# Four-strip bias table products ahead of the transposes, and a new order of dilated loads and first values, in a hybrid decoder step on one Trainium2 core

## The reference, cut to what matters

```python
h = rms_norm(x, norm_attn); proj = h @ w_in          # 2840 columns
bias = rel_bias[t5_bucket(distance)]                 # (32, 16 heads), log buckets
# mixer A, sample rows: windows (128, 1), (512, 4), (2048, 16) over the cached keys and values
logits = q . k * scale + bias; probs = masked_softmax(logits); out = probs @ v
# mixer B, sample rows: compressed blocks -> top 16 blocks -> gathered keys and values -> softmax -> @ v
x = x + concat(A, B) @ w_out; y = final_norm(x + conv_ffn(rms_norm(x, norm_ffn)))
```

## Time and profile before

| what | value |
|---|---|
| median of 3 runs | 2094.52 us (2089.33 to 2097.07) |
| the profiled execution | 2091.84 us |
| its span | 2090.0 us |
| TensorE busy | 2030.1 us (97%), 12334 matmul records |
| VectorE, ScalarE, POOL busy | 53%, 25%, 28% |
| DMA | 373.04 MB moved, 178 GB/s on average |

### The profile page before, as it was taken

How to read it: one execution, slowest core, us unless ns; L and a number is a source line. 1 busy time by engine, 2 the same in 40 slices (tenths; PEclk the granted TensorE clock), 3 DMA queues, 4 the chain that set the end, 5 groups by cost and what they waited for, 6 DMA issues and landing times. The chain is left out here.

```text
span 2090.0 us, 31740 instructions
## 1 busy us (share of the span) xinstructions
PE 2030.1 (97%) x12334; PEld 1325.8 (63%) x12334; DVE 1113.5 (53%) x2524; ACT 520.4 (25%) x1140; POOL 578.9 (28%) x753
## 2 busy tenths in 40 slices
PE   7999999999989989999999999999999999999998
PEld 3445466666556666766776458888888888634443
DVE  4035455421535546777775467777776766511452
ACT  4111010101333435776675031111111111000001
POOL 2444234202025740112232441322222222304110
PEclk9999999999999999999999999999999999999999
DMA  9376677663699994233343126666665422601111
GB/s 255 118 237 258 263 289 277 242 214 124 229 365 387 419 409 162 70 92 92 93 143 112 29 81 221 221 211 213 218 205 202 142 81 62 242 4 30 43 40 41
DMA packets 154296, 373.04 MB, mean 178 GB/s; under 512 B 34885, under 2 KB 92989, under 8 KB 136093
## 3 DMA queue, kind: packets, MB, share of 16 engines
q1 hardware_dynamic: 126420, 149.63, 22.8%
q0 software_dynamic: 25472, 149.45, 18.4%
q10 hardware_dynamic: 2256, 71.94, 9.8%
HBM read 343.68 MB, written 98.60 MB: 212 GB/s over the span
## 5 line engine op out<-in xcount | busy, mean ns | idle before, releaser
L2981 PE MATMUL ff_ps<-ff_hx,whole_aw 128*128 128x264 f32 x2464 | 550.5, 386 | 0.8 <-DVE ff_hx L3377 0.8
L2981 PEld LDWEIGHTS ff_ps<-ff_hx,whole_aw 128*128 128x128 f32 x2464 | 467.1, 190 | 80.6 <-issue 1.2
L837 DVE STREAM_TRANSPOSE whole_space<-whole_space 128x512 f32<-128x512 f32 x256 | 155.3, 674 | 153.6 <-PE late_bank L637 153.6
L601 PE MATMUL late_bank<-in_w,in_xT 128*128 128x512 f32 (+1 forms) x512 | 201.6, 547 | 0.0
L1224 DVE CUSTOM_DVE_ANT_0 pa_L<-late_bank,whole_space 128x512 f32<-128x512 f32 (+3 forms) x288 | 141.0, 532 | 43.4 <-PE late_bank L1070 41.8
L601 PEld LDWEIGHTS late_bank<-in_w,in_xT 128*128 128x128 f32 x512 | 95.1, 191 | 95.0 <-issue 88.4
L1196 ACT ACTIVATE pa_L<-pa_L,pa_nm 128x640 f32<-128x640 f32 (+3 forms) x192 | 142.0, 741 | 47.0 <-DVE pa_nm L1236 46.7
L3007 PE MATMUL ff_ps<-ff_hx,whole_space 128*128 128x512 f32 x336 | 148.0, 593 | 0.0
L717 ACT ACTIVATE in_yout<-late_bank 128x128 f32<-128x128 f32 (+5 forms) x88 | 40.9, 479 | 380.7 <-PE late_bank L601 200.2
L3461 DVE SCALAR_TENSOR_TENSOR whole_space<-whole_space,ff_kept 128x1024 f32<-128x1024 f32 x88 | 123.1, 1399 | 3.1
L637 PE MATMUL late_bank<-whole_space 128*64 128x256 f32 (+1 forms) x1152 | 121.6, 364 | 0.0
(11 more groups left out here) (441 smaller groups left out, 2670.0 us busy)
## 6 DMA issues: line engine op xcount, KB each, us to landing
out_new_a_k_s<-in_cache_a_k ACTq DMA_DIRECT2D x8, 4088.0 KB
out_new_a_v_s<-in_cache_a_v ACTq DMA_DIRECT2D x8, 4088.0 KB
whole_aw<-in_w_up SPq DMA_DIRECT2D x44, 512.0 KB, 7.4
in_w<-in_w_in SPq DMA_DIRECT2D x5, 2048.0 KB, 13.0
whole_space<-in_cache_a_k SPq DMA_DIRECT2D x8, 1024.0 KB
whole_space<-in_cache_a_v SPq DMA_DIRECT2D x8, 1024.0 KB
ff_hx<-in_w_down SPq DMA_DIRECT2D x14, 512.0 KB, 4.2
whole_space<-in_x_prompt SPq DMA_DIRECT2D x12, 512.0 KB, 10.2
```

The lines of the kernel that those rows point to most:

```text
L601: mm = pe.matmul(ps[0:n, b, 0:width], xT[:, k, t * P:t * P + n], w[:, at % WBUF, k, 0:width], start=(k == 0), stop=(k == KC - 1))
L837: last = dve.transpose(put[:, dh, :, k * HD:k * HD + HD].rearrange("p t (g b) -> p t g b", g=2), got[:, :, :, dh, :])
L2981: mm = pe.matmul(ps[:, bank_of(x, j, g), 0:H2], aw[:, j % 2, at, k, :], hx[:, bt, k, g * H2:g * H2 + H2], start=(k == 0), stop=(k == KH - 1))
```

## The change

The 13 table products become four jobs. Job m takes the chunks m, m+4, m+8, m+12, each on its own strip of 32 columns (the stationary matrix is padded with zero columns to 32, which POOL fills), so a job gives up to 128 x 512 values, copied out at once. All four stand ahead of the x jobs. The tables are stored in six pieces in place of three. ScalarE now copies the first half of every tile, and both halves of tiles 2, 5 and 8. VectorE copies the second half of the others.

In the dilated stage `probs(0)` moves from the end of step 5 to the end of step 4 on all three engines, and `values(0)` from the start of step 6 to between `keys(5, 0)` and `scores(4, 1)`. The values semaphore is raised for each sequence. SP's order of loads is 5, 7, 8, 9, 10, 6, 11 to 15, then the choice; window values are loaded when the keys of sequence 6 are used, ahead of the window keys. POOL issues the first two gathers when the first half's values are multiplied (before: when all keys were transposed), and the next two after the fifth sequence's values.

```diff
-    shares = [chunks[0:5], chunks[5:9], chunks[9:13]]
-    jobs = []
-    for g in range(NG):
-        jobs += [("b", i, c) for i, c in shares[g]]
-        for t in range(3 * g, 3 * g + 3):
-            jobs += [("x", t, 0), ("x", t, 1)]
+    NBJ = 4
...
+    jobs = [("b", m) for m in range(NBJ)]
+    first_x = len(jobs)
+    for t in range(NTILE):
+        jobs += [("x", t, 0), ("x", t, 1)]
...
-    on_act = [j >= NX or j % 2 == 0 for j in range(NJ)]
+    def by_act(j):
+        if j < first_x:
+            return j % 2 == 0
+        return j >= NX or jobs[j][2] == 0 or jobs[j][1] % 3 == 2
...
-        relx = m.sb("relx", [35, 3, HA + HB])
+        relx = m.sb("relx", [35, 3, 32])
...
+            for i, c, j, at, n in segments:
+                name = tables[i][0]
+                o = (A0 if name == "tabS" else 0) + c * CH
+                sp.dma_start(scr[name][:, o:o + n * CH],
+                             res[32 * j:32 * j + HA + HB, at * CH:at * CH + n * CH]).then_inc(s_ts, 16)
...
+                        pe.wait_ge(s_one, 3)
+                    for k in range(job[1], len(chunks), NBJ):
+                        i, c = chunks[k]
+                        o, strip = tables[i][1] + c * CH, k // NBJ * 32
+                        mm = pe.matmul(ps[strip:strip + 32, b, :], relx[:, i, :], tab_op[:, o:o + CH], start=True, stop=True,
+                                       tile_position=(0, strip))
...
             root(0)
             moved(0)
+            moved(2)
+            turned(0, 0)
             squares(3)
+            turned(1, 0)
             squares(4)
-            moved(2)
             squares(5)
-            moved(4)
             root(1)
-            for j in (6, 8, 10):
-                moved(j)
+            turned(2, 0)
+            turned(2, 1)
+            turned(3, 0)
             squares(6)
-            moved(12)
+            turned(4, 0)
             squares(7)
             squares(8)
...
+            moved(1)
             mean_square(0)
-            for t in range(3):
-                scaled(t)
-            moved(1)
+            scaled(0)
             moved(3)
+            scaled(1)
+            turned(0)
+            scaled(2)
+            turned(1)
             mean_square(1)
...
+            pool.memset(relx[:, :, HA + HB:32], 0.0).then_inc(s_one, 1)
```

The dilated stage:

```diff
+        turning = (4, 9)
...
-                if s == 5 + 4 * g:
+                if s == turning[g]:
...
-            pool.wait_ge(d_tr, use["keys", NB - 1, NTL - 1] + 1)
-            pool.wait_ge(d_pv, 1)
+            pool.wait_ge(d_pv, 4)
             for c in range(2):
                 pre.gather_keys(pool, 0, c)
+            pool.wait_ge(d_tr, use["keys", NB - 1, NTL - 1] + 1)
             ahead.retire()
             pool.sem_inc(ops.s_retired, 1)
-            pool.wait_ge(d_pv, 2)
+            pool.wait_ge(d_pv, 5)
...
-            for i in range(5, 12):
+            for i in (5, 7, 8, 9, 10, 6, 11, 12, 13, 14, 15):
...
-            for i in range(12, 16):
-                load(i)
...
+            sp.wait_ge(d_tr, use["keys", NB - 2, NTL - 1] + 1)
+            pre.load_window(sp, "cache_win_v", pre.value, pre.s_wv)
             sp.wait_ge(d_tr, use["keys", NB - 1, NTL - 1] + 1)
             pre.load_window(sp, "cache_win_k", pre.key, pre.s_wk)
...
-            pre.load_window(sp, "cache_win_v", pre.value, pre.s_wv)
...
-                mm.then_inc(d_pv, 1)
+                    mm.then_inc(d_pv, 1)
...
             for s in range(NB + 4):
+                if s == 10:
+                    values(1)
                 for g in range(2):
-                    if s == 6 + 4 * g:
-                        values(g)
                     if s == 7 + 4 * g:
                         out(g)
                 if s < NB:
                     keys(s, 0)
+                if s == 5:
+                    values(0)
```

More of the change, by code:

```diff
@@ L294, in front @@
     span_of = {ch: [j for j, x in enumerate(jobs) if x[0] in "nsq" and x[1] == ch] for ch in range(6)}
-    first_x = {g: min(j for j, x in enumerate(jobs) if x[0] == "x" and x[1] == 3 * g) for g in range(NG)}
     last_b = max(j for j, x in enumerate(jobs) if x[0] == "b")
@@ L299, in front @@
     kT_row = {0: 0, 2: 8, 3: 10}
-    on_act = [j >= NX or j % 2 == 0 for j in range(NJ)]
+    def by_act(j):
+        if j < first_x:
+            return j % 2 == 0
+        return j >= NX or jobs[j][2] == 0 or jobs[j][1] % 3 == 2
+    on_act = [by_act(j) for j in range(NJ)]
     def done(j):
@@ L690, in copy_out @@
             if job[0] == "b":
-                _, i, c = job
-                o = res_at[i] + c * CH
-                return copy(res[:, o:o + CH], ps[0:HA + HB, b, :], 1.0)
+                n = 32 * len(range(job[1], len(chunks), NBJ))
+                return copy(res[0:n, job[1] * CH:job[1] * CH + CH], ps[0:n, b, :], 1.0)
             if job[0] == "x":
@@ L755, in _, with turned @@
             nc.scalar.activation(bias[:, 0:1], bias[:, 0:1], ACT.Sqrt)
+            def turned(t, h):
+                moved(first_x + 2 * t + h)
             squares(0)
@@ L856, in _, with turned @@
             dve.wait_ge(s_one, 2)
+            def turned(t):
+                moved(first_x + 2 * t + 1)
+            moved(1)
             mean_square(0)
-            for t in range(3):
-                scaled(t)
-            moved(1)
+            scaled(0)
             moved(3)
+            scaled(1)
+            turned(0)
+            scaled(2)
+            turned(1)
             mean_square(1)
-            for t in range(3, 6):
-                moved(2 * t - 1)
-                scaled(t)
-            moved(11)
-            moved(13)
-            mean_square(2)
-            for t in range(6, 9):
-                moved(2 * t + 3)
-                scaled(t)
-            for j in range(21, NX, 2):
-                moved(j)
+            scaled(3)
+            scaled(4)
+            turned(3)
+            scaled(5)
+            turned(4)
+            mean_square(2)
+            scaled(6)
+            scaled(7)
+            turned(6)
+            scaled(8)
+            turned(7)
             indices()
@@ L1426, in free_after @@
             g, kv, j = turns[i]
-            return (d_tr, use["keys", g * 4 + j, NTL - 1] + 1) if kv == 0 else (d_pv, g + 1)
+            return (d_tr, use["keys", g * 4 + j, NTL - 1] + 1) if kv == 0 else (d_pv, 4 * g + j + 1)
         LOADS = 16 * 9
```

45 lines of the change are left out of this document (23 added, 22 removed).

## The result

The changed kernel took 2100.24 us in the median of 8 runs, the kernel before 2094.75 in the median of 8: ratio 1.0033, 95% interval [1.0016, 1.0049], so 3.4 to 10.3 us more, 5.5 between the medians. The forecast was 2094.5, no change. The result lies inside the range of 2084 to 2103 and within 0.5%, but it is a loss that the measurement tells from nothing. The profiled execution took 2096.91 us, span 2095.1 (before: 2091.84 and 2090.0); it is the fastest of the eight, so its waits may be shorter than most.

What follows compares the result with a forecast made beforehand. TensorE was taken to bound the kernel except in the selected branch, where DMA is full. Minus 2.8 us (opening) plus 2.8 (half the dilated stage's 5.6) left 2091.8 for the profiled execution, median 2094.5, range 2084 to 2103.

Steps and rivals of the forecast that it cites:

- The opening: Start to first projection: four table rounds in 7.3 us, first projection at 37.9 in place of 40.74, minus 2.8 us.
- The stalls: Dilated stage, steps 5 and 6: TensorE waits for VectorE's moved work, plus 2.2 and 3.4 us; half, 2.8, reaches the end.
- The loads: Load queues around the dilated stage: earlier values gain 0, loads 12 to 15 do no harm, early gathers only change order.
- the load queue turns against it: SP's queue: choice behind loads 12 to 15 makes window keys land at 623.6, 4 us late; 2101.3 us; chance 0.2.
- the prefetch pays: Selected stage: VectorE's work finds cover, two gathers leave the full stretch, 5 us less; 2086.7 us; chance 0.27.

Runs made afterwards that it cites:

- first kernel: The kernel before with only the opening's part of the change, old dilated stage and queues: ratio 0.9996 to the kernel before.
- 17: The kernel before with the opening's part and ScalarE's squares ahead of its queued copies, old dilated stage and load queues: 0.9969, 2083.66 us.
- twelfth kernel: The changed kernel with window values loaded after the mix stores and gathers by the old rules, stalls kept: ratio 1.0008 to the kernel before.
- tenth: The changed kernel with only the window values loaded after the mix stores again: ratio 1.0003 to the kernel before.
- sixteenth: The changed kernel with the two window loads swapped, keys first, values right behind, both ahead of the mix stores: ratio 1.0006 to the kernel before.
- third kernel: The changed kernel with the choice stored ahead of item 14, not behind item 15: ratio 1.0011 to the kernel before.
- sixth: The changed kernel with both VectorE stalls removed and the choice stored ahead of item 12: ratio 1.0017 to the kernel before.
- eighth: The changed kernel with the first half's turning and values at their old places and the choice stored ahead of item 12: 1.0038 to the kernel before.
- fourteenth: The sixth kernel with window values loaded after the mix stores, early gathers kept: ratio 0.9958 to the kernel before.
- thirteenth: The sixth kernel with window values after the mix stores and gathers by the old rules: ratio 0.9985 to the kernel before.
- fifteenth kernel: The fourteenth kernel with ScalarE's squares ahead of its queued copies in the opening: ratio 0.9941 to the kernel before, 2080.5 us.

## Why the prediction was wrong

**The opening** was right in its mechanism. Predicted: tables in 7.3 us, second and third groups scaled from 24.2 and 31.6, first projection at 37.9. Measured: 7.04, 24.26 and 31.37, and 37.58. A round of three strips (6 records, 1.70 us) cost no more than one of four (8 records, 1.93). Thirteen products of 1.74 us one after the other would be 22.6, so 7.04 is 3.2 times faster. By the 2.38 of the Trainium skill ("TensorE: Matmul & The Clock Gate", Part 3, measured speedup) the tables would have taken 8.4, an estimate (so they would have ended near 18.3 and not 18.7, a slip of the prediction); the trace of this float32 kernel disagrees with it. Two things were luckier than they look. The prediction calls the first products as slow as the low clock makes them, yet the granted clock of 9.93 to 18.64 reads 1.00 in the kernel before; the durations carried the sum, not the clock row. And 37.58 is one of thirteen executions between 37.07 and 39.73; the gain of 2.8 was mean 2.4 over executions. That it passes through to the end was taken for granted; the first kernel has 0.8 with an interval that holds both, and only with the squares ahead (17) is a gain at the end clear.

**The stalls** were right in place and size: 2.2 and 3.4 predicted, 2.58 and 3.17 measured. That half of them, 2.8, reaches the end was a choice between bounds; the twelfth kernel's 2.5 agrees with it, but its doubt of some 5 us covers none and all as well.

**The step that failed is "The loads".** It walks through the values of sequences 1 to 3, items 12 to 15 and the gathers, and leaves out the fourth thing that the diff moves on SP's queue: the window values, from behind the mix stores to ahead of the window keys. The sentence with which the load-queue rival was turned down, that with a shorter backlog the keys should land in 10 us, was a sound number for another kernel: it is what the tenth and sixteenth show, 9.3 and 8.5. With 2 MB put ahead of them it was 21.3. The swap alone measures 0.0027 of the ratio, 5.6 us (some 5 of doubt either way), which is the distance of 5.7 between forecast and result; with it, and all else of the change in place, the sixteenth kernel is at 1.0006, the forecast's no change. So what the sum lacked was a term for the window keys, and no term in it was clearly mis-sized.

**The rival "the load queue turns against it"**, given a chance of 0.2, had late window keys and nearly every number: choice stored near 588 (587.14), landed near 598 (595.98), window keys out near 602 (598.70), landing 623.6 (620.0), a wait of 4 us (3.69), time 2101.3 (2100.24). Part of that was luck: its 21.6 us to landing came from a queue with a full backlog, while here SP's stand-still had let the backlog run out (DMA share 0.66 in 590 to 600) and the 21.3 came from the values ahead; without them the same issue took 8.5. It blamed SP's wait for the choice. Storing the choice earlier mends it in the third kernel, whose keys have landed by 615.1 while the stalls hold TensorE until 617, but not in the sixth and eighth, where TensorE is ready at 610.5 and 613.0. So in the changed kernel either edit removes the wait; where TensorE has no stalls, only the place of the window values does (fourteenth against sixth: keys landed by 607.2 against 618.9).

**The rival "the prefetch pays"** was turned down since "the hole is only moved". That is true of the hole and was still the wrong conclusion, though the changed kernel hides it: once the window keys are in time, the early gathers are worth 5.6 us (fourteenth against thirteenth), where the rival had 2 x 2.6 = 5.2. The closeness is partly luck, since the thirteenth's branch of 183.0 us is unusually long; against the 180.2 of the kernel before the branch is 2.6 shorter. With no stalls, the choice stored earlier and one load put back, the rest of the change pays: the fourteenth kernel is at 0.9958.

That DMA issued by POOL and by SP share the same engines, as the Trainium skill has it ("DMA: Bandwidth & Descriptors", "Issuing engines are not separate DMA queues"), the tenth and twelfth kernels bear out, which differ in POOL's gathers alone: with two of them issued at 592.20 and 593.51, just ahead of SP's window keys at 594.75, the keys take 13.8 us to land, without them 9.3.

Left open: how much of the loss is the granted clock. Of the kernel before, in the first set of runs, nine executions with a mean clock of 0.992 took 2089.7 us on average and five with 0.988 took 2095.2; the changed kernel had 0.986 to 0.989. A stopped TensorE and a lower clock come together here, and no run separates them. Also open: why the thirteenth kernel, which starts the window part 2.7 us earlier than the kernel before, ends the selected branch no earlier (794.16 against 794.02), while the first kernel ends it 4.1 earlier. Not tried: the fifteenth kernel with the window values directly behind the keys.

## What to carry to other kernels

List every transfer that a diff moves, with what it is moved ahead of on its queue, and ask of each one overtaken when it is needed: bytes that nobody waits for soon must not stand ahead of bytes that somebody does. Where a late load holds the buffer that the next transfers need, its lateness is paid twice, by the waiting engine and by a longer stage behind it (here 4.0 and 3.1 us), and it can swallow gains made upstream. If removing a stall moves nothing, look for the wait downstream that grew by the same amount.

## What the runs showed of the hardware

The stretch 34.9 to 44.4 of one and the same code was granted 0.50, 0.60 and 1.00 of the clock in three executions, and the first projection job took 3.64, 3.40 and 1.92 us; from first table product to first projection the three executions differ by up to 2.4 us. The issue of the same two window-key loads took SP 1.23 us in the changed kernel and 6.71 in the sixth, where it came earlier in the backlog: an issue was no fixed cost on this queue. The time from issue to landing was none either: the same two loads took 8.5 us in the sixteenth kernel, and 16.7 and 22.5 in the fourteenth and thirteenth, where no window values stood ahead of them either but items 12 to 15 had just been issued.
